# A weight's low part in pieces of 256 columns, and weights split over their own size only

## The reference

```python
# first block: latent attention, gated short convolution, attention to 256 memory rows
proj = rmsnorm(x, norm_g) @ w_in
q = (rmsnorm(q_lat, q_norm_g) @ w_uq); kv = (rmsnorm(kv_lat, kv_norm_g) @ w_ukv)   # 8 heads, rope
mkv = rmsnorm(mem, mem_norm_g) @ w_mkv                                             # 4 heads
y = r_attn * (o_attn @ w_br_attn) + r_conv * (o_conv @ w_br_conv) + r_mem * (o_mem @ w_br_mem)
x = x + y @ w_out
# second block: stick-breaking attention (16 heads) + MLP, then HGRN2 recurrence (8 heads) + MLP
x = x + stick_breaking_mixer(rmsnorm(x), w_qkv, w_o)
x = x + relu(rmsnorm(x) @ w1) ** 2 @ w2
x = x + hgrn2_mixer(rmsnorm(x), w_in, w_o)
x = x + relu(rmsnorm(x) @ w1) ** 2 @ w2
```

## Time and profile before

| What | Value |
|---|---|
| Median of three runs | 2004.3 us |
| Lowest and highest | 2002.17 and 2006.76 us |
| The profiled execution, its own time | 2006.44 us |
| Its span in the profile | 2004.3 us |
| Granted clock of TensorE, mean | 0.99 of 2.4 GHz |
| Busy: TensorE, VectorE, GpSimd, ScalarE | 1958.3, 974.2, 748.6, 705.0 us |

### The profile page before, as it was taken

The page is one execution under the profiler, slowest core; times in us unless marked ns, Lnnn a source line. Parts: engine busy times, 40 slices in busy tenths (PEclk is TensorE's granted clock), DMA queues, the critical chain, the costliest instruction groups (busy, mean ns, idle before and its releaser), DMA issues.

```text
span 2004.3 us, 25097 instructions
## 1 busy us (share of the span) xinstructions
PE 1958.3 (98%) x9928; PEld 1595.7 (80%) x9928; DVE 974.2 (49%) x1670; ACT 705.0 (35%) x1129; POOL 748.6 (37%) x308
## 2 busy tenths in 40 slices
PE   7998999999999999999999999999999999999998
PEld 5877777788888877767888888878888888888886
DVE  6648775732225476775522333254755555233332
ACT  4445444543333355564222222232222232222221
POOL 3216222356664322214444444422222145444441
PEclk9989999999999999999999999989999999999999
DMA  6214122223333211112333333222212133333331
GB/s 171 64 33 116 46 59 55 53 69 95 97 104 108 85 53 54 56 41 79 100 95 95 95 95 95 84 74 73 61 56 63 43 85 105 95 95 95 95 95 53
DMA packets 269142, 159.63 MB, mean 80 GB/s; under 512 B 6137, under 2 KB 267489, under 8 KB 269026
## 3 DMA queue, kind: packets, MB, share of 16 engines
q1 hardware_dynamic: 269026, 158.02, 27.3%
HBM read 155.91 MB, written 2.10 MB: 79 GB/s over the span
## 4 chain that ended last, share of the span: by engine, by line
PE 92%; DVE 5%; ACT 1%; issue 1%; DMA 0%; POOL 0%; SPq 0%; ACTq 0%; DVEq 0%
PE bank L244 35%; PE bank L707 6%; PE bank L708 6%; PE bank L709 6%; PE bank L2320 3%; PE bank L2322 3%; PE bank L2321 3%; PE bank L2351 3%; PE bank L1673 3%; PE bank L509 2%; PE bank L1675 2%; PE bank L1674 2%; PE bank L511 2%; PE bank L510 2%; PE bank L879 1%; PE bank L1723 1%
## 5 line engine op out<-in xcount | busy, mean ns | idle before, releaser
L227 POOL TENSOR_TENSOR weight_lo<-weight_stage,weight_hi 128x1024 fp32r<-128x1024 f32 x303 | 748.1, 2474 | 1225.5 <-ACT weight_hi L217 1225.2
L217 ACT ACTIVATE weight_hi<-weight_stage 128x1024 fp32r<-128x1024 f32 x303 | 319.7, 1056 | 326.3 <-PE bank L244 256.7
L2071 DVE TENSOR_TENSOR x_t<-x_t,bank 128x512 f32<-128x512 f32 x128 | 82.3, 684 | 266.7 <-PE bank L244 266.7
L244 PE MATMUL bank<-hidden_hi,weight_lo 128*128 128x512 f32 x512 | 201.9, 394 | 0.0
L707 PE MATMUL bank<-a_hi,weight_lo 128*128 128x512 f32 (+1 forms) x464 | 199.6, 430 | 2.3 <-DVE a_lo_rounded L1211 2.1
L244 PE MATMUL bank<-hidden_hi,weight_hi 128*128 128x512 f32 x512 | 201.8, 394 | 0.0
L244 PE MATMUL bank<-hidden_lo,weight_hi 128*128 128x512 f32 x512 | 201.8, 394 | 0.0
L244 PE MATMUL bank<-a_hi,weight_lo 128*128 128x512 f32 x512 | 199.7, 390 | 0.0
L244 PE MATMUL bank<-a_lo_rounded,weight_hi 128*128 128x512 f32 x512 | 199.3, 389 | 0.0
L244 PE MATMUL bank<-a_hi,weight_hi 128*128 128x512 f32 x512 | 199.2, 389 | 0.0
L708 PE MATMUL bank<-a_lo_rounded,weight_hi 128*128 128x512 f32 (+1 forms) x464 | 184.0, 397 | 0.0
(11 more groups left out here) (341 smaller groups left out, 3557.2 us busy)
## 6 DMA issues: line engine op xcount, KB each, us to landing
weight_stage<-in_mlp_w SPq DMA_DIRECT2D x128, 512.0 KB, 3.9
weight_stage<-in_w_in SPq DMA_DIRECT2D x57, 512.0 KB, 3.8
weight_stage<-in_hg_w_in SPq DMA_DIRECT2D x32, 512.0 KB, 4.0
weight_stage<-in_sb_w_qkv SPq DMA_DIRECT2D x24, 512.0 KB, 3.8
weight_stage<-in_w_mkv SPq DMA_DIRECT2D x8, 512.0 KB, 3.8
weight_stage<-in_w_out SPq DMA_DIRECT2D x8, 512.0 KB, 3.8
weight_stage<-in_sb_w_o SPq DMA_DIRECT2D x8, 512.0 KB, 3.8
weight_stage<-in_hg_w_o SPq DMA_DIRECT2D x8, 512.0 KB, 3.8
```

The costliest lines, as they stand in the source:

```text
L217: act.activation(self.hi[slot][:, :], self.stage[slot][:, :], ACT.Copy).then_inc(self.hi_done, 1)
L227: pool.tensor_tensor(self.lo[slot][:, :], self.stage[slot][:, :], self.hi[slot][:, :].bitcast(F32), ALU.subtract).then_inc(self.split_done, 1)
L244: last = pe.matmul(out, l, r, start=n == 0, stop=n == 3 * len(pairs) - 1)
L2071: dve.tensor_tensor(S.x[:, t, :], S.x[:, t, :], S.ps[4 + r % 2 * 2 + m][:, :], ALU.add).then_inc(added, 1)
```

## The change

ScalarE rounds only the columns that the unit has. GpSimd makes the low part of a unit in pieces of 256 columns, again only over the unit's size: four instructions for 1024 columns, three for 768, two for 512. The semaphore `split_done` is raised by the last piece. Nothing else changes: the order of the programs, the loads and the products are the same.

```diff
+PIECE = 256
...
-        act.activation(self.hi[slot][:, :], self.stage[slot][:, :], ACT.Copy).then_inc(self.hi_done, 1)
+        size = self.units[c][1]
+        act.activation(self.hi[slot][:, 0:size], self.stage[slot][:, 0:size], ACT.Copy).then_inc(self.hi_done, 1)
...
             pool.wait_ge(self.hi_done, u + 1)
-            pool.tensor_tensor(self.lo[slot][:, :], self.stage[slot][:, :], self.hi[slot][:, :].bitcast(F32),
-                               ALU.subtract).then_inc(self.split_done, 1)
+            for a in range(0, size, PIECE):
+                part = slice(a, min(a + PIECE, size))
+                last = pool.tensor_tensor(self.lo[slot][:, part], self.stage[slot][:, part],
+                                          self.hi[slot][:, part].bitcast(F32), ALU.subtract)
+            last.then_inc(self.split_done, 1)
```

## The result

| | before | after |
|---|---|---|
| Median of seven runs each | 2006.61 us | 1993.6 us |
| Lowest and highest | 2002.17 and 2007.13 us | 1988.72 and 1997.5 us |
| Profiled execution, its own time | 2006.4 us | 1993.6 us |
| Its span | 2004.3 us | 1991.5 us |

The kernel is faster by 0.57%: the ratio is 0.9943, with a 95% interval of 0.993 to 0.9957. The median lies 3.2 us under the forecast 1996.8. Between the two profiled executions 12.8 us are saved, where the sum said 7.5. In the changed kernel the lines from the low part on stand six or seven lower: L227 is now L233, L879 L886, L918 L925, L1066 L1073.

The account below looks back on a forecast made before the run. TensorE was taken as the bound, busy 1958.3 of 2004.3 us. Terms 1.0 - 0.8 + 1.5 + 1.5 + 3.0 + 1.5 - 1.2 + 1.0 saved 7.5: 1998.9, less 2.1 for the median, 1996.8; range 1991 to 2005.

Parts of the forecast that it names:

- The price of a piece: GpSimd's low part: 256 columns take 0.74 us alone with 0.20 fixed (upper bound 0.40), 1.15 in turns with VectorE.
- the largest rival: Pieces nearly free (0.6 us) and the clock kept up: 13.0 us saved in all, 1991.3 us; chance 0.10.
- Part 1: Start: first unit 0.6 us later, 1.6 back by the sums of squares; net 1.0 saved (-0.7 to +2.5).
- Part 2: Third unit of the query projection: splitting 3.4 us for 2.4, rounding shorter; net 0.8 lost (0 to -1.3).
- Part 3: Memory keys and values, 155 to 192 us: VectorE's chain earlier, GpSimd's units later; +1.5 us waits, +1.5 clock.
- Part 4: Gates, 358 to 415 us: five held low parts end earlier, saving 3.0 us (0 to 3.8).
- Parts 5 and 7: End of stick breaking, +1.5 of 1.9 us waited; recurrence, one hold on the chain, +1.0 us.
- Part 6: Output projection after stick breaking, first units: wait 1.6 us becomes 2.8, so -1.2; -4 if the clock falls.
- One more sign: Anywhere in the kernel, no VectorE operation with two SBUF inputs was to take above 1.4 us.
- Part 8: Fewer columns in 24 units of the mix stage and 4 others: saves nothing, TensorE has no gap there.
- the hold only moves: Next chain operation meets the next piece; gates, stick breaking, recurrence give nothing: 2002.3 us; chance 0.27 with another small case.
- The slower rival: GpSimd's queued next piece goes first, VectorE held a whole unit: 14 us slower, 2018; slower outcomes had chance 0.11.

Follow-up runs that it names:

- size alone: Changed kernel with each low part in one instruction over the unit's own size: 2003.8 us, ratio 0.9996 to the kernel before.
- pieces elsewhere: Changed kernel with pieces only in the mix, output projections, multilayer parts and units 0 and 14, whole units otherwise: 2008.9 us, ratio 1.0019.
- pieces where held: Changed kernel with pieces only in the first block up to the gates (not units 0, 14), stick breaking and recurrence: 1992.1 us, ratio 0.9936.
- whole units where awaited: Changed kernel with six units that TensorE waits for split whole: 1991.2 us, ratio 0.9935; second run 1993.5 us, 0.9939.
- pieces alone: Changed kernel with pieces of 256, but every unit rounded and split over all 1024 columns: 1996.9 us, ratio 0.9958.
- memory stage undone: Changed kernel with units 16 to 25, the memory stage's, split whole: 1995.8 us, ratio 0.9959.
- gates undone: Changed kernel with units from the gates to the first of the mix split whole: 1996.7 us, ratio 0.9967.

## Why the prediction was right, and where a step was off

**The price of a piece held.** The least durations of GpSimd's instruction, one per run, are 0.308 us for 64 columns, 0.442 for 128, 0.716 for 256, 1.280 for 512 and 2.344 for 1024. From one to the next this is 2.1 to 2.2 ns a column, and a fixed part of about 0.17, where 0.20 was taken from memset and ScalarE. The bound of 0.40 never came near. Its rows, for the changed kernel:

```profile
L233 POOL TENSOR_TENSOR weight_lo<-weight_stage,weight_hi x1160: 716/737/1392, 10.3 to 1961.1; 128x256 fp32r<-128x256 f32 x194
```

The Trainium skill's estimate from GPSIMD Engine Reference, section 3.1 (2.09 ns a column and 0.22 fixed), is confirmed within 0.05 us a piece, so its rule against the change was right in size, and too small to decide.

**Where pieces follow one another** they are a little cheaper than alone, as at the start:

```profile
10.28 2.78 POOL L233 TENSOR_TENSOR weight_lo<-weight_stage,weight_hi 128x256 fp32r<-128x256 f32 x4 [9.34 <-ACT weight_hi L221]
```

That is 0.695 us each, and the 897.5 us that the page counts as busy are less than 1160 times its mean of 806 ns, since the records of neighbours overlap. The Trainium skill, GPSIMD Engine Reference, section 2.1 (a core goes on to its next instruction when its own share is done), agrees with this. It is worth 0.02 to 0.04 us a piece, far from the 0.15 of the largest rival.

**Part 1, the start, was mis-sized.** Net 1.0 was forecast with 2.5 as the upper bound, and it gave 2.8. The first unit costs 0.4. The sums of squares, for which TensorE waits in both kernels, end 2.8 us earlier (31.1 for 34.0), where the forecast had 1.6: they take 8.08 us for 9.78 and begin 1.1 earlier, since work before them was held less too. Another 1.6 us is a dip of the clock at 65 to 85 us (0.91 before, 1.00 after), and that doesn't belong to the change: size alone and pieces elsewhere have 1.00 there too, and 0.91 is found again with pieces where held and in the second run with whole units where awaited.

**Part 2 held**: 4.3 us before the query head against 4.5 forecast, worked out as three pieces and turns; the fourth piece and the longer rounding of the run with pieces alone cost another 1.2.

**Part 3 held in its mechanism.** The wait at L879 was to fall under 2 and is gone; in its place come waits for weight_lo at L714 (L707 before), two of the three inside 160 to 183 us. The chain ends at 171.4 for the forecast 174.9, and the stage had begun 3.5 us earlier: the turns took what was forecast. Two sizes were off. TensorE came to the first score 2.6 us later against the rest of its program, where the forecast had 3.2 and 0.5 more for the newton steps; the stand of 5.2 us for the exponents went wholly, as forecast: 2.8 instead of 1.5. And half of the clock's loss was taken to come back; nearly all of it did (2.8 of 3.0), since after the new stands, 1.3 us at most, the clock is 1.00.

**Part 4 went past its bound.** The point forecast, 3.0, was what TensorE was seen to wait at L918, the bound 3.8; the stage gave 4.3, and undoing it cost 3.8. TensorE's windows from the same matmul to the same matmul, of before and then of after:

```profile
354.00:414.20 60.20, 57.12 (x288) 1.00 0.21 56
```

```profile
344.80:400.80 56.00, 56.00 (x289) 1.00 0.21 53
```

The stands were 3.1 us, as the waits say, and are gone. The other 1.1 us is busy time, at a granted clock of 1.00 in both. The step that failed is "TensorE can take back only what it waits". The timeline of TensorE before shows what a stand costs beyond its idle time:

```profile
368.45 0.39 PE L708 MATMUL bank<-a_lo_rounded,weight_hi 128*128 128x512 f32 x1
368.68 0.40 PE L709 MATMUL bank<-a_hi,weight_hi 128*128 128x512 f32 x1
369.30 0.44 PE L918 MATMUL bank<-const,first_work 128*128 128x128 f32 x2 [0.22 <-DVE first_work L1144]
```

Without a wait the next matmul starts 0.23 us after the last, while that one is recorded for 0.40; idle time is counted from its recorded end. So the start at 369.30 is 0.62 behind the one before it, where the changed kernel has 0.24: 0.38 lost for a recorded wait of 0.22. Matched one by one, the six starts that waited lost 0.05 to 0.17 more each than their idle time, 0.75 in all; one more came 0.13 late with no idle time recorded, and the rest of the 1.1 is smaller. Undoing the stage brought 3.8 back, again more than L926's 2.8. The mechanism is the one forecast: the low part at 365 us of 2.88 is 1.22, and the column operations behind it meet a piece for 0.1 and 0.4 us (they take 0.16 and 0.35 alone), where the forecast had 0.2 and 0.5. The timeline of the gates:

```profile
356.16 1.22 DVE L1073 TENSOR_TENSOR q_heads_rounded<-kv_heads,q_heads_rounded 128x512 fp32r<-128x512 f32 x1
357.75 0.25 DVE L1144 TENSOR_TENSOR first_columns<-first_columns 128x1 f32<-128x1 f32 x1
...
358.11 0.71 DVE L1151 TENSOR_SCALAR first_work<-first_work,first_columns 128x256 f32<-128x256 f32 x1
```

**Parts 5 and 7 held**: 1.6 for 1.5 and 0.9 for 1.0, with the weights' product at 1.26 us for 2.90.

**Part 6 held in its wait and not in its clock.** The wait is 2.5 us for the forecast 2.8. In the timeline of TensorE:

```profile
907.47 0.50 PE L516 MATMUL bank<-sb_o_hi,weight_lo 128*128 128x512 f32 x1 [2.54 <-POOL weight_lo L233]
```

The forecast named -4 if the clock fell after such a stand, and took the case that it doesn't. It fell in part: 1.6 us, so that this part costs 2.5 and not 1.2. This is one of the forecast's own signs of being wrong, a clock that falls where it stood at 1.00, and it was met. The stand doesn't settle it, though: the traces with the memory stage undone and with pieces elsewhere have the same stand of 2.6 us there, and 1.00 behind it. With the memory stage undone:

```profile
900.00:925.00 25.00, 22.45 (x100) 1.00 0.29 80
```

The output projection after the recurrence, built alike, was not in the sum at all; it costs 0.7. One more sign fails in the letter: six instructions of VectorE stand above 1.4 us, all L1845 in stick breaking at 1.48, of which 0.95 is their own.

**Part 8 held**: size alone can't be told from no change, and the mix stage, where ScalarE and GpSimd do less, moves TensorE nowhere.

**The rivals.** That the hold only moves is refuted by the gates and by the recurrence; it is true only in the newton steps, where it costs nothing at 256 and 5 us at 512. The slower rival has no place at 256: VectorE gets its turn, 1.13 us long, after each piece, as it did after each unit before. The Trainium skill, SBUF — State Buffer, section "SBUF: two separate sides", says that who starts first keeps the shared ports for the whole instruction; the trace agrees (2.25 us on two columns). Its rule does not say who comes next when both have work, and the runs with 128 and 64 show that it isn't always VectorE. The largest rival is nearest in time (1991.3 for 1993.6, where the forecast had 1996.8), and only half of its reason is found: the clock was kept, but pieces were not free, and the gates gave more. So the forecast was right in what makes the gain and in its range, and its sum was 5 us short: parts 1, 3 and 4 together were 5.7 us too small, 1.6 came from the clock's dip that isn't the change's, and 2.3 go off for the clock in part 6 and for the second output projection.

## What to carry to other kernels

Where GpSimd and VectorE both read SBUF and only one of them is near the critical path, cut the instructions of the other so that a turn is short, and price the cut by its fixed part (0.17 us here) times the pieces, at the units that TensorE waits for. Don't cut too fine: at 512 of 1024 columns a chain of tiny instructions still paid 1.2 us a link, at 256 it was best, and at 128 the gain was gone. In the list of waits look at what follows a long stand too: as much came back in the memory stage through the clock (2.8 us) as through the stands.

## What was not expected of the hardware

- VectorE can be passed over between GpSimd's instructions when these are short: for 8.49 and 3.94 us beside pieces of 128 columns, for over 2 us fourteen times beside pieces of 64. With 256, 512 and 1024 columns, none had more than two begin while it stood.
- Instructions on 32 columns or fewer stand for a whole piece like large ones: 0.65 us beside 256, 1.2 beside 512, 0.39 beside 128, each with 0.16 to 0.19 alone.
- After a stand of 2.5 us in the output projection the granted clock was 0.93 over 25 us in four traces (the change twice, pieces alone, gates undone) and 1.00 in two (memory stage undone, pieces elsewhere). After one of 1.6 in the same place it was 1.00, both before the change and with whole units there. So the length of a stand doesn't decide alone.
